# Delta-rule scan: gram products on alternating 64-row halves of TensorE, a padded state operand and one state product per head pair

## The chip, the core and the metric

One core of one Trainium2 chip runs the whole program. The metric is the device time of one execution in microseconds, as the median of several runs.

## The reference, cut to what matters

The program is one inference step of a two-layer model over 640 tokens (128 context tokens and 512 latent tokens, width 1024): layer 0 mixes with a gated linear recurrence, layer 1 with RWKV-7 time mixing, and each layer ends with a mixture of experts. Only the scan of layer 1 is touched. For each of 16 heads of width 64, and in both directions (forwards and backwards over the tokens), it computes the delta rule:

```python
def rwkv7_scan(r, w, k, v, kk, a, s0):
    def step(s, inp):
        r_t, w_t, k_t, v_t, kk_t, a_t = inp
        sa = jnp.einsum('bhvk,bhk->bhv', s, -kk_t)
        s = s * w_t[:, :, None, :] + sa[..., None] * (kk_t * a_t)[:, :, None, :] + v_t[..., None] * k_t[:, :, None, :]
        return s, jnp.einsum('bhvk,bhk->bhv', s, r_t)
```

The kernel computes it in chunks of 128 tokens. Within a chunk the recurrence becomes two masked 128x128 matrices per head and operand pair (gram products of decayed keys, rates and queries), a triangular inverse, and products with the state at the start of the chunk.

## The kernel before

**Tiling of the scan.** Heads are taken in 4 groups `g` of 4 heads (`HG`), which is 2 pairs (`UC`) of 64-wide heads, so that a pair fills 128 partitions: head 0 of a pair lies in partitions 0 to 63, head 1 in 64 to 127. For each group, 5 chunks `st` are taken in order (`st` 0 is the context chunk, which starts from a zero state and has no state product), and in each of these 20 steps both directions `d` are worked on in turn. The loop `for g ... for st` stands three times, once for each engine: TensorE from L980, VectorE from L1981, ScalarE from L1386.

**One step on TensorE**, in program order, always for d = 0 and then d = 1:

- AR (L984) and BR (L992): the gram products. `z["BE"]` or `z["KP"]` (a pair's 128 partitions) is the stationary operand, the moving one is `RHS4`, 512 columns for each pair: head 0's 256 columns hold zeros in partitions 64 to 127, head 1's hold zeros in partitions 0 to 63. A contraction over 128 rows thus gives each head its own product. Two matmuls of 512 columns for a tile.
- AN (L999): bonus sums and the transposes of `KP` and `BE`.
- M0 (L1017): transposes of `N`, and then for levels 1 to 6 the tiles G and D (L1021 to L1047), which build the inverse by doubling. After the G tiles of level 2, `gate_tiles` (L966) makes the gates of the next step: four matmuls that contract over the 64 rows of direction `d`, then one of 256 columns with `bones` over all 128 rows.
- N6 (L1048, transposes), RHS (L1052), Us (L1065), OT (L1074). For `st` > 0, RHS and OT each hold one state product for every head: 128 rows, with the zero halves of `RHS4` as stationary operand and `R0` (64 columns for each pair) as moving one.

**PSUM ring.** There are four PSUM tiles (`RING_P` = 4) that are used in turn. `open_tile(n)` (L661) waits until the reader has freed tile n - 4. M0 for d = 0 therefore takes the place of BR for d = 0, and waits until VectorE has masked that (L2004).

**VectorE in a step**: the mask of AR (L1991) and two operations on `N` (L1997, L1998), for both directions; the masks of BR (L2004); the bonus sums (L2013); `R0` from `ST` (L2016); then the G masks (L2028) and D updates (L2044) of the levels, with the preparation of the next step's operands between and after them, the last of which is `decayed_operands` (L1940), which fills `RHS4` with four operations on 64 partitions. At the end of the step, after each OT tile, it brings up the state (L2071, L2073 or, for `st` 0, L2080), adds the output (L2085) and, from group 1 on, runs `gn_apply` (L1970). All of these stand in one queue in this order.

**ScalarE** copies the transposed tiles (L1393, L1397, L1404, L1429) and computes the gates' exponentials (L1351 and after).

Of the kernel before, what the change touches and what calls it, by code (L numbers as in the profile page):

```python
# [15 lines left out]
P = 128  # L16
D = 1024
KT = D // P
# [23 lines left out]
HG = 4  # L42
# [103 lines left out]
def build(nc, A, const, outs, xspill, slots_in, slots_out):  # L146
# [9 lines left out]
    with ctx:  # L156
# [275 lines left out]
        for d in range(2):  # L432
            z = {}
            for name, n in (("LA", 2 * UW), ("B", UW), ("E1", UW), ("E2", UW), ("E3", UW), ("KK", UW), ("SQ", UW),
                            ("BE", UW), ("KP", UW), ("RHS4_0", 4 * UW), ("RHS4_1", 4 * UW), ("KBT", 2 * UW),
                            ("AR", HG * 256), ("BR", HG * 256), ("M", HG * P), ("N", HG * P), ("G", HG * HD),
                            ("RHU", 2 * HG * HD), ("R0", UC * HD), ("SF", UC * HD)):
# [132 lines left out]
        def _(pool):  # L570
# [87 lines left out]
        def _(pe):  # L658
# [307 lines left out]
            def gate_tiles(g, st):  # L966

                for d in range(2):
                    z, ch, uid = STR[d], chunk_of(st, d), unit_id(g, st, d)
                    lo, ts = slice(HD * d, HD * d + HD), slice(ch * P, (ch + 1) * P)  # L970
                    ps = open_tile(T[f"P_{g}_{st}"] + d)
                    for q, (w2, hid) in enumerate(((W2s, hw), (A2s, ha))):
                        for j in range(UC):
                            ct = UC * g + j
                            mm(ps[:, (UC * q + j) * P:(UC * q + j + 1) * P], w2[lo, ct * P:(ct + 1) * P], hid[lo, ts])
                    pe.wait_ge(S["kk_sq"], uid + 1)
                    done(mm(ps[:, 2 * UW:3 * UW], bones, z["SQ"]))

            gate_tiles(0, 0)
            for g in range(NGRP):  # L980
                for st in range(NCH):
                    u = f"_{g}_{st}"
                    rh = f"RHS4_{(g * NCH + st) % 2}"
                    for d in range(2):  # L984
# [3 lines left out]
                        for j in range(UC):  # L988
                            ins = mm(ps[:, 512 * j:512 * j + 512], z["BE"][:, j * P:(j + 1) * P],
                                     z[rh][:, 512 * j:512 * j + 512])  # L990
                        done(ins)
                    for d in range(2):  # L992
                        z = STR[d]
                        ps = open_tile(T["BR" + u] + d)
                        for j in range(UC):
                            ins = mm(ps[:, 512 * j:512 * j + 512], z["KP"][:, j * P:(j + 1) * P],
                                     z[rh][:, 512 * j:512 * j + 512])
                        done(ins)
# [53 lines left out]
                    for d in range(2):  # L1052
# [3 lines left out]
                        ps = open_tile(T["RHS" + u] + d)  # L1056
# [1129 lines left out]
```

## Time and profile before

| | |
|---|---|
| median of 3 runs | 3113.26 us (3071.8 to 3114.75) |
| span of the profiled execution | 3100.0 us |
| TensorE busy | 2596.5 us, 84% of the span |
| VectorE busy | 1236.9 us, 40% |
| ScalarE busy | 785.9 us, 25% |
| mean granted TensorE clock | 0.902 |
| the 20 steps of the scan (1495.66 to 2620.1 us) | 1124.44 us |

Busy time is counted for each engine on its own. "PE" is TensorE's matmul side, "PEld" its weight loads, which overlap the matmuls, "DVE" is VectorE, "ACT" ScalarE. In a row of the timeline, "x8" is the number of instructions merged into it, and a bracket at its end is the idle time of the engine before it with what released it. "issue" in a bracket means that the profile shows nothing that was waited for. [...]

### The profile page before, as it was taken

How to read it: one execution, taken by the hardware profiler on the slowest of the kernel's cores; microseconds unless marked ns; L12 is line 12 of the kernel's file. 1: busy time of each engine (PE TensorE's matmuls, PEld its weight loads, DVE VectorE, ACT ScalarE, POOL GpSimd, SP SyncE). 2: the span in 40 equal slices, each digit the busy share in tenths (PEclk: the TensorE clock that was granted, in tenths of full speed). 3: DMA queues.
4: the chain of work that ended last, by engine and by line, in shares of the span. 5: the costliest groups of instructions: out<-in, count | busy, mean ns of one | idle time of the engine just before them, and what ended most of it. 6: DMA issues, size and time to landing. Idle time of an engine off the chain costs nothing.

```text
span 3100.0 us, 35206 instructions
## 1 busy us (share of the span) xinstructions
PE 2596.5 (84%) x14506; PEld 1969.5 (64%) x14506; DVE 1236.9 (40%) x2688; ACT 785.9 (25%) x1570; POOL 158.7 (5%) x178
## 2 busy tenths in 40 slices
PE   6999905488899835997799999999999998968974
PEld 3544705455566523556688889888888887556653
DVE  2254126622111116100666665666566665221104
ACT  2253212302011102001334343344243342020111
POOL 2000003400100010001000000000000000000001
PEclk9999956688899967999899997999899999969987
DMA  6144180005699732221000000000000000048962
GB/s 222 55 136 155 56 352 4 2 16 181 232 324 325 229 138 91 68 68 53 3 3 1 1 3 1 1 1 3 1 1 1 3 1 35 28 154 272 346 210 108
DMA packets 202299, 300.99 MB, mean 97 GB/s; under 512 B 12180, under 2 KB 170112, under 8 KB 201760
## 3 DMA queue, kind: packets, MB, share of 16 engines
q1 hardware_dynamic: 180096, 225.62, 22.1%
q0 software_dynamic: 11984, 40.63, 3.5%
q10 hardware_dynamic: 10064, 32.51, 2.6%
q8 instruction: 117, 1.92, 0.3%
q14 instruction: 38, 0.31, 0.0%
HBM read 237.39 MB, written 61.35 MB: 96 GB/s over the span
## 4 chain that ended last, share of the span: by engine, by line
PE 75%; DVE 12%; ACT 3%; DMA 3%; issue 2%; ACTq 2%; POOL 2%; SPq 0%; POOLq 0%; DVEq 0%
PE psum_ring L677 68%; PE psum_ring L1013 4%; DMA arena<-expert_inputs 1%; PE psum_ring L767 1%; ACTq L1263 1%; ACT h_normed L1158 1%; ACTq L1260 1%; ACT arena L1351 1%; DVE arena L1991 1%; DVE x_resid L1991 1%; DVE x_resid L2004 1%; DVE arena L2004 1%; POOL arena L633 1%; POOL expert_inputs L621 1%; DVE h_normed L1829 1%
## 5 line engine op out<-in xcount | busy, mean ns | idle before, releaser
L677 PE MATMUL psum_ring<-arena 128*128 128x64 f32 (+4 forms) x5200 | 982.4, 339 | 54.6 <-ACT arena L1173 17.5
L677 PEld LDWEIGHTS psum_ring<-arena 128*128 128x128 f32 (+1 forms) x5200 | 762.2, 197 | 214.6 <-issue 132.5
L677 PE MATMUL psum_ring<-x_resid 128*128 128x64 f32 x2368 | 334.2, 281 | 0.0
L677 PEld LDWEIGHTS psum_ring<-x_resid 128*128 128x128 f32 x2368 | 306.4, 199 | 0.0
L677 PE MATMUL psum_ring<-arena,weight_ring 128*128 128x512 f32 (+1 forms) x832 | 230.3, 438 | 5.6 <-DVE arena L1804 3.4
L677 PE MATMUL psum_ring<-h_normed,weight_ring 128*128 128x512 f32 (+1 forms) x768 | 211.7, 437 | 5.8 <-ACT h_normed L1158 5.8
L677 PEld LDWEIGHTS psum_ring<-arena,weight_ring 128*128 128x128 f32 x832 | 127.9, 193 | 107.4 <-issue 102.6
L677 PEld LDWEIGHTS psum_ring<-h_normed,weight_ring 128*128 128x128 f32 x768 | 117.8, 192 | 98.9 <-issue 98.8
L677 PE MATMUL psum_ring<-weight_ring,small 128*2 128x256 f32 x768 | 171.9, 382 | 0.0
L677 PE MATMUL psum_ring<-h_normed 128*128 128x128 f32 x190 | 43.4, 411 | 117.5 <-DVE h_normed L1829 98.0
L677 PEld LDWEIGHTS psum_ring<-weight_ring,small 128*2 128x2 f32 x768 | 63.7, 85 | 108.6 <-issue 15.3
L767 PE MATMUL psum_ring<-consts,arena 128*128 128x128 f32 x350 | 56.5, 299 | 90.5 <-DMA arena<-expert_inputs 87.7
L677 PEld LDWEIGHTS psum_ring<-h_normed 128*128 128x128 f32 x190 | 39.3, 311 | 121.6 <-issue 87.9
L767 PEld LDWEIGHTS psum_ring<-consts,arena 128*128 128x128 f32 x350 | 45.6, 154 | 110.2 <-DMA arena<-expert_inputs 90.8
L677 PE MATMUL psum_ring<-x_resid,weight_ring 128*128 128x512 f32 (+1 forms) x320 | 89.9, 444 | 25.7 <-DVE x_resid L1873 25.7
L1183 ACT ACTIVATE arena<-psum_ring 128x256 f32<-128x256 f32 x32 | 12.3, 384 | 368.6 <-PE psum_ring L677 368.6
L1013 PE MATMUL psum_ring<-consts,arena 128*128 128x128 f32 x560 | 91.4, 288 | 14.6 <-DVE arena L2044 14.3
L1404 ACT ACTIVATE arena<-psum_ring 128x512 f32<-128x512 f32 x100 | 59.4, 594 | 170.1 <-PE psum_ring L677 170.1
L1393 ACT ACTIVATE arena<-psum_ring 128x512 f32<-128x512 f32 x40 | 23.9, 598 | 296.8 <-PE psum_ring L1008 296.8
L1013 PE MATMUL psum_ring<-consts,x_resid 128*128 128x128 f32 x560 | 90.9, 287 | 9.3 <-DVE x_resid L2004 9.2
L621 POOL DMA_INDIRECT expert_inputs<-arena x20 | 19.5, 975 | 1476.9 <-DVE arena L1599 1471.4
L1616 DVE TENSOR_TENSOR arena<-arena,psum_ring 128x256 f32<-128x256 f32 x32 | 13.5, 421 | 202.1 <-ACT arena L1183 202.1
(346 smaller groups left out, 3316.8 us busy)
## 6 DMA issues: line engine op xcount, KB each, us to landing
arena<-in_moe_w SPq DMA_DIRECT2D x105, 1024.0 KB, 11.2
weight_ring<-in_w_mod SPq DMA_DIRECT2D x48, 1024.0 KB, 5.4
arena<-expert_inputs SPq DMA_DIRECT2D x35, 512.0 KB, 8.1
expert_outputs<-arena POOLq DMA_DIRECT2D x32, 512.0 KB, 7.8
weight_ring<-in_ab_w_in SPq DMA_DIRECT2D x14, 1024.0 KB, 5.0
expert_inputs<-arena ACTq DMA_DIRECT2D x1, 12800.0 KB, 36.8
expert_outputs<-arena ACTq DMA_DIRECT2D x1, 12800.0 KB, 67.3
weight_ring<-in_ab_w_out SPq DMA_DIRECT2D x4, 1024.0 KB, 6.4
```

The costliest lines, as they stand in the source:

```text
L621: pool.indirect_dma_start(slots_in, bass.IndirectOffsetOnAxis(ap=PI[:, j * NCH + c:j * NCH + c + 1], axis=0), HTOK[:, c, :], None).then_in ...
L633: pool.indirect_dma_start((G0, G1)[j][:, c, :], None, slots_out, bass.IndirectOffsetOnAxis(ap=PI[:, j * NCH + c:j * NCH + c + 1], axis=0)) ...
L677: return nc.tensor.matmul(out, lhsT, rhs, start=start, stop=stop)
L767: ins = nc.tensor.transpose(ps[:, k * P:(k + 1) * P], src[:, k * P:(k + 1) * P], ident)
L1013: ins = nc.tensor.transpose(ps[:, c0 + hl * P:c0 + (hl + 1) * P], src[:, hl * P:(hl + 1) * P], ident)
L1158: A_(H[:, k, a:b], H[:, k, a:b], ACT.Identity, scale=coef[i][:, 2 * k + s:2 * k + s + 1], bias=MOD[:, layer, shift + k, s:s + 1]).then_inc ...
L1260: act.dma_start(dst.rearrange("(a p) d -> p a d", p=P), ZERO.unsqueeze(1).broadcast_to([P, NE + N_OVER, D])).then_inc(S["zero_filled"], 16)
L1263: act.dma_start(outs["rglru"][0, 0].rearrange("d (c p) -> (d c) p", p=P), LROWS[0:8, 0:P]).then_inc(S["lru_sent"], 16)
L1351: ins = A_(z["LA"][:, c0:c0 + P], ps[:, c0:c0 + P], ACT.Exp, scale=-1.0, bias=nb[:, bi:bi + 1])
L1404: A_(STR[d]["N"], ps[:, 512:512 + HG * P], ACT.Copy).then_inc(S["n_out"], 1)
L1991: free(TT(z["AR"].rearrange("p (h c) -> p h c", c=256), ps.rearrange("p (h c) -> p h c", c=256), m, ALU.mult), n)
L2004: free(TT(z["BR"].rearrange("p (h c) -> p h c", c=256), ps.rearrange("p (h c) -> p h c", c=256), m, ALU.mult), n)
```

## The change

- **Operands.** `RHS4_q` (four 128-column parts for each pair, half of it zeros) becomes `RHS_q` (two parts, no zeros). `decayed_operands` fills it with two operations on 128 partitions in place of four on 64.
- **Gram products** (AR, BR). New `gram`: for each pair and each head of it one matmul that contracts over the head's own 64 rows, 256 columns; the calls alternate between rows 0 to 63 and 64 to 127. Head 0's products go to the first PSUM bank of the tile and head 1's to the second, and `masked_gram` on VectorE puts them back in head order as it masks.
- **Gates.** The 64-row matmuls of both directions alternate, and the two `bones` products follow.
- **State products.** `R0` now holds 128 columns for each pair, block-diagonal, with zeros written once by GpSimd. RHS and OT have one state product of 128 columns for each pair in place of one of 64 columns for each head.
- **State on VectorE.** `R0` from `ST`, and `ST` from `R0`, are each two operations on 64 partitions in place of one on 128. GpSimd clears two small tiles in place of four large ones.

```diff
@@ STR tiles
-  ("RHS4_0", 4 * UW), ("RHS4_1", 4 * UW), ... ("R0", UC * HD)
+  ("RHS_0", 2 * UW), ("RHS_1", 2 * UW), ... ("R0", HG * HD)
@@ gpsimd
-                for q in range(2):
-                    nc.gpsimd.memset(STR[d][f"RHS4_{q}"], 0.0).then_inc(S["rw_clear"], 1)
+                nc.gpsimd.memset(STR[d]["R0"], 0.0).then_inc(S["rw_clear"], 1)
@@ tensor, gate_tiles
+                pt = [open_tile(T[f"P_{g}_{st}"] + d) for d in range(2)]
+                for q, (w2, hid) in enumerate(((W2s, hw), (A2s, ha))):
+                    for j in range(UC):
+                        ct = UC * g + j
+                        for d in range(2):
+                            ch = chunk_of(st, d)
+                            lo, ts = slice(HD * d, HD * d + HD), slice(ch * P, (ch + 1) * P)
+                            mm(pt[d][:, (UC * q + j) * P:(UC * q + j + 1) * P], w2[lo, ct * P:(ct + 1) * P],
+                               hid[lo, ts])
                 for d in range(2):
...
+                    pe.wait_ge(S["kk_sq"], unit_id(g, st, d) + 1)
+                    done(mm(pt[d][:, 2 * UW:3 * UW], bones, STR[d]["SQ"]))
+
+            def gram(ps, left, right):
+
+                for j in range(UC):
+                    for hh in range(2):
+                        k = slice(HD * hh, HD * hh + HD)
+                        c0 = (hh * UC + j) * 256
+                        ins = mm(ps[:, c0:c0 + 256], left[k, j * P:(j + 1) * P], right[k, j * 256:(j + 1) * 256])
+                return ins
@@ tensor, AR (BR with z["KP"] alike)
-                        for j in range(UC):
-                            ins = mm(ps[:, 512 * j:512 * j + 512], z["BE"][:, j * P:(j + 1) * P],
-                                     z[rh][:, 512 * j:512 * j + 512])
-                        done(ins)
+                        done(gram(ps, z["BE"], z[rh]))
@@ tensor, RHS (OT alike, with columns P to 2P of the pair's part)
+                        for j in range(UC if st else 0):
+                            mm(ps[:, j * P:(j + 1) * P], z[rh][:, j * 256:j * 256 + P], z["R0"][:, j * P:(j + 1) * P],
+                               j == 0, False)
                         for hl in range(HG):
...
-                            if st:
-                                mm(out, z[rh][:, hl * 256:hl * 256 + P], z["R0"][:, (hl // 2) * HD:(hl // 2 + 1) * HD],
-                                   True, False)
-                            ins = mm(out, z["BR"][:, hl * 256:hl * 256 + P], V1[:, ch, hv], st == 0, True)
+                            ins = mm(out, z["BR"][:, hl * 256:hl * 256 + P], V1[:, ch, hv], st == 0 and hl == 0,
+                                     hl == HG - 1)
@@ vector, decayed_operands
-                for hh in range(2):
-                    pr = slice(HD * hh, HD * hh + HD)
-                    TT(r5[pr, :, hh, 0, :], c3(z["KK"])[pr], c3(z["E3"])[pr], ALU.mult)
-                    ins = TT(r5[pr, :, hh, 1, :], R1[pr, cg, ts], c3(z["E1"])[pr], ALU.mult)
-                ins.then_inc(S["unit_ready"], 1)
+                r4 = z[f"RHS_{(g * NCH + st) % 2}"].rearrange("p (j a t) -> p j a t", j=UC, a=2)
+                TT(r4[:, :, 0, :], c3(z["KK"]), c3(z["E3"]), ALU.mult)
+                TT(r4[:, :, 1, :], R1[:, cg, ts], c3(z["E1"]), ALU.mult).then_inc(S["unit_ready"], 1)
@@ vector, masks of AR and BR
+            def masked_gram(dst, ps, d):
+
+                m = CO[:, C_RMASK + 256 * d:C_RMASK + 256 * d + 256]
+                m = m.unsqueeze(1).unsqueeze(1).broadcast_to([P, 2, UC, 256])
+                return TT(dst.rearrange("p (j h c) -> p h j c", h=2, c=256),
+                          ps.rearrange("p (h j c) -> p h j c", h=2, c=256), m, ALU.mult)
@@ vector, end of a step (R0 from ST is split in the same way)
-                            link(TT(ST[:, KT * d + UC * g:KT * d + UC * (g + 1), :], r0,
-                                    eb.unsqueeze(2).broadcast_to([P, UC, HD]), ALU.mult))
+                            for pr, r0 in state_halves(d):
+                                ins = TT(ST[pr, KT * d + UC * g:KT * d + UC * (g + 1), :], r0,
+                                         eb[pr].unsqueeze(2).broadcast_to([HD, UC, HD]), ALU.mult)
+                            link(ins)
```

## Rows read from the trace of the kernel before

**Rows 1.** The page: busy time of each engine, its share of the span, and instructions.

```profile
PE 2596.5 (84%) x14506; PEld 1969.5 (64%) x14506; DVE 1236.9 (40%) x2688; ACT 785.9 (25%) x1570; POOL 158.7 (5%) x178
```

**Rows 2.** Windows, one scan step each: stretch and length, busy engines, PEclk, DMA, GB/s.

```profile
1819.71:1888.56 68.85, 66.73 (x415) 61.70 (x413) 35.36 (x87) 21.68 (x53) 0.00 (x0) 0.78 0.01 3
1888.56:1952.76 64.20, 62.03 (x415) 56.85 (x414) 36.05 (x90) 21.75 (x53) 0.00 (x0) 0.84 0.00 1
1952.76:2009.20 56.44, 54.25 (x414) 48.92 (x414) 35.77 (x90) 21.65 (x53) 0.00 (x0) 0.97 0.00 1
...
2171.12:2240.20 69.08, 66.91 (x415) 61.73 (x414) 36.04 (x90) 21.75 (x53) 0.00 (x0) 0.78 0.00 1
...
2349.80:2402.35 52.55, 49.68 (x387) 44.22 (x386) 36.04 (x91) 21.65 (x53) 0.00 (x0) 1.00 0.01 1
...
2456.94:2511.74 54.80, 52.61 (x415) 47.28 (x414) 35.67 (x90) 21.65 (x53) 0.00 (x0) 1.00 0.01 1
...
sum 1124.44, PE 1080.40 PEld 973.75 DVE 695.70 ACT 419.68 POOL 0.00; mean PE 54.02 PEld 48.69 DVE 34.78 ACT 20.98 POOL 0.00
```

**Rows 3.** Timeline of TensorE, end of one step (N6, OT) and start of the next.

```profile
2498.30 0.66 PE L1013 MATMUL psum_ring<-consts,arena 128*128 128x128 f32 x4
...
2504.59 4.01 PE L677 MATMUL psum_ring<-arena 128*128 128x128 f32 x34
...
2511.74 7.08 PE L677 MATMUL psum_ring<-arena 128*128 128x512 f32 x16
2518.66 0.50 PE L677 MATMUL psum_ring<-consts,arena 128*128 128x2 f32 x4
...
2520.42 0.63 PE L1013 MATMUL psum_ring<-consts,arena 128*128 128x128 f32 x4
2521.55 0.63 PE L1013 MATMUL psum_ring<-consts,x_resid 128*128 128x128 f32 x4 [0.50 <-DVE x_resid L2004]
```

**Rows 4.** Timeline of VectorE over the same step boundary.

```profile
2511.94 0.58 DVE L2071 TENSOR_TENSOR x_resid<-x_resid,psum_ring 64x128 f32<-64x128 f32 x2 [2.21 <-PE psum_ring L677]
2512.56 0.29 DVE L2073 TENSOR_TENSOR arena<-x_resid,small 128x128 f32<-128x128 f32 x1
...
2513.89 1.22 DVE L1991 TENSOR_TENSOR arena<-psum_ring,consts 128x1024 f32<-128x1024 f32 x1
...
2519.06 1.22 DVE L2004 TENSOR_TENSOR arena<-psum_ring,consts 128x1024 f32<-128x1024 f32 x1
2520.20 1.21 DVE L2004 TENSOR_TENSOR x_resid<-psum_ring,consts 128x1024 f32<-128x1024 f32 x1
...
2521.65 0.28 DVE L2016 TENSOR_TENSOR arena<-arena,small 128x128 f32<-128x128 f32 x1
```

**Rows 5.** Timeline of TensorE around the gate tiles of one step.

```profile
1836.00 1.16 PE L677 MATMUL psum_ring<-arena 64*128 64x128 f32 x8
1837.09 0.70 PE L677 MATMUL psum_ring<-arena,consts 128*128 128x256 f32 x2
1837.72 1.16 PE L677 MATMUL psum_ring<-arena 64*128 64x128 f32 x8
...
1841.98 0.66 PE L1013 MATMUL psum_ring<-consts,arena 128*128 128x128 f32 x4 [0.75 <-DVE arena L2044]
```

**Rows 6.** Timeline of TensorE before and after a stretch at the lower clock.

```profile
1850.06 1.07 PE L677 MATMUL psum_ring<-arena 128*128 128x64 f32 x8 [0.91 <-issue]
...
1880.07 5.35 PE L677 MATMUL psum_ring<-arena 128*128 128x128 f32 x34
```

**Rows 7.** Windows (columns as in rows 2): stretches at the lower clock, the first ahead of the scan.

```profile
1473.00:1480.00 7.00, 6.86 (x34) 5.77 (x34) 1.97 (x4) 1.14 (x4) 0.00 (x0) 0.50 0.02 5
1495.66:1500.60 4.94, 4.94 (x6) 2.19 (x7) 3.28 (x7) 0.00 (x0) 0.00 (x0) 0.50 0.00 0
...
1852.10:1882.90 30.80, 30.80 (x150) 30.74 (x148) 14.47 (x41) 6.63 (x16) 0.00 (x0) 0.50 0.00 1
```

**Rows 8.** Timeline of TensorE ahead of the scan, within the first stretch of rows 7.

```profile
1474.90 2.02 PE L677 MATMUL psum_ring<-arena 64*128 64x128 f32 x8
```

More of the change, by code:

```diff
@@ L982, in _ @@
                     u = f"_{g}_{st}"
-                    rh = f"RHS4_{(g * NCH + st) % 2}"
+                    rh = f"RHS_{(g * NCH + st) % 2}"
                     for d in range(2):
@@ L994, in _ @@
                         ps = open_tile(T["BR" + u] + d)
[L995 to L998, printed above, removed]
+                        done(gram(ps, z["KP"], z[rh]))
                     for d in range(2):
@@ L1084, in _ @@
                                False, True)
+                        for j in range(UC if st else 0):
+                            mm(ps[:, j * P:(j + 1) * P], z[rh][:, j * 256 + P:(j + 1) * 256],
+                               z["R0"][:, j * P:(j + 1) * P], j == 0, False)
                         for hl in range(HG):
@@ L1087, in _ @@
                             hv = slice((HG * g + hl) * HD, (HG * g + hl + 1) * HD)
-                            mm(out, z["BR"][:, hl * 256 + P:(hl + 1) * 256], V1[:, ch, hv], True, False)
+                            mm(out, z["BR"][:, hl * 256 + P:(hl + 1) * 256], V1[:, ch, hv], st == 0 and hl == 0, False)
                             ins = mm(out, z["AR"][:, hl * 256 + P:(hl + 1) * 256], z["U"][:, hl * HD:(hl + 1) * HD],
-                                     False, st == 0)
-                            if st:
-                                ins = mm(out, z[rh][:, hl * 256 + P:(hl + 1) * 256],
-                                         z["R0"][:, (hl // 2) * HD:(hl // 2 + 1) * HD], False, True)
+                                     False, hl == HG - 1)
                         done(ins)
@@ L1880, in _ @@
             read_out(dve, T["stT"] + 1)
-            dve.wait_ge(S["rw_clear"], 6)
+            dve.wait_ge(S["rw_clear"], 4)
             def c3(a):
@@ L1979, in _, with state_halves @@
                     stage(0, 0, d)
+            def masked_gram(dst, ps, d):
[3 more added lines that the diff above has]
+                          ps.rearrange("p (h j c) -> p h j c", h=2, c=256), m, ALU.mult)
+            def state_halves(d):
+                r4 = STR[d]["R0"].rearrange("p (j h v) -> p j h v", h=2, v=HD)
+                return [(slice(HD * hh, HD * hh + HD), r4[HD * hh:HD * hh + HD, :, hh, :]) for hh in range(2)]
             idb = ident.unsqueeze(1).broadcast_to([P, HG, P])
@@ L2065, in _ @@
                         tt = ps[:, 512:512 + UC * P].rearrange("p (j c) -> p j c", c=P)
-                        r0 = z["R0"].rearrange("p (j v) -> p j v", v=HD)
                         eb = em[:, par + 2 * d:par + 2 * d + 2]
                         if st:
-                            for hh in range(2):
-                                pr = slice(HD * hh, HD * hh + HD)
-                                ins = TT(r0[pr], r0[pr], tt[pr, :, HD * hh:HD * hh + HD], ALU.add)
+                            for hh, (pr, r0) in enumerate(state_halves(d)):
+                                ins = TT(r0, r0, tt[pr, :, HD * hh:HD * hh + HD], ALU.add)
                             link(ins)
-                            link(TT(ST[:, KT * d + UC * g:KT * d + UC * (g + 1), :], r0,
-                                    eb.unsqueeze(2).broadcast_to([P, UC, HD]), ALU.mult))
+                            for pr, r0 in state_halves(d):
+                                ins = TT(ST[pr, KT * d + UC * g:KT * d + UC * (g + 1), :], r0,
+                                         eb[pr].unsqueeze(2).broadcast_to([HD, UC, HD]), ALU.mult)
+                            link(ins)
                         else:
```

30 lines of the change are left out of this document (8 added, 22 removed).

## The prediction

> **What bounds the kernel now.** I read the page first. TensorE is busy for 84% of the span and VectorE for 40% [rows 1], so this is a TensorE kernel as a whole. The whole says little about the change, which touches only the 20 steps of the scan. I therefore cut the scan into its steps with the windows view [rows 2]. The reader is to see two things there. A step at the full clock takes 54.8 us from group 1 on (52.55 for the context chunk), of which TensorE is busy for 52.6. And four steps are longer, in step with a lower mean clock: 68.85, 64.20, 56.44 and 69.08 us. Against 54.8 these lose 14.05 + 9.40 + 1.64 + 14.28 = 39.4 us. All 20 steps sum to 1124.4 us.
>
> Next the timelines of TensorE and VectorE over one step boundary [rows 3, 4]. On TensorE the gram products run from 2511.74 to 2518.66, 6.92 us. On VectorE the last output tile of the old step is taken up at 2511.94, and from there its queue has no pause: the state, the output, group normalisation, the mask of AR from 2513.89, the work on N, the other direction, and the first mask of BR from 2519.06, which ends at 2520.28. M0 on TensorE starts at 2520.42, since it needs that PSUM tile. So two chains of nearly equal length end at M0: TensorE's own (grams and AN, 8.7 us) and VectorE's. The second M0 already waits 0.50 us for VectorE [rows 3]. This is what decides the worth of faster grams.
>
> **The change, part by part.** The sum is made against the span of 3100.0 us; the median of the runs, 3113.3, stands 13.3 above it, and I add that at the end.
>
> *State products.* OT of both directions is 64 MATMUL instructions in 7.15 us (2504.59 to 2511.74, rows 3), 0.112 us each, and these are 64 and 128 columns alike, so I price a wider one the same. For each step with `st` > 0, RHS goes from 32 instructions to 24 and OT from 64 to 56. That is 16 x 0.112 = 1.79 us a step, on a stretch where TensorE never waits, and 16 such steps give 28.6 us.
>
> *VectorE at the end of a step.* `ST` is written by two operations. One costs 0.29 [rows 4], a half has as many elements for each partition of its own, so 0.29 more. It stands in the queue ahead of the mask of AR, so M0 comes 0.29 later, 8.97 us after the grams start in place of 8.68: 15 steps, 4.4 us lost. In group 0 there is no group normalisation ahead of the mask, and I take nothing there. `R0` from `ST` becomes four operations in place of two (0.28 each, rows 4). They lie while TensorE does the second M0 and the first G tiles (from 2521.55, about 1.4 us), which covers them; uncovered they would cost 0.6 a step. `decayed_operands` saves four operations a step, in a place where VectorE next waits 2 to 3 us for OT: nothing. GpSimd's clears end ahead of the first gate tile: nothing.
>
> *Gram products, the doubtful term.* 16 instructions of 512 columns become 32 of 256. If the halves of the array don't overlap, they take 6.9 us as now. If they overlap fully, 3.5. No row of before has matmuls on alternating halves. [...] I take 5.1 us, near the middle. A change between 64-row and 128-row matmuls costs about 0.2: eight 64-row ones take 1.09 us to the next kind [rows 5], 8 x 0.112 is 0.90. What the grams save then goes nowhere, for M0 waits for VectorE at 8.97 us: the saved 1.6 us become idle time. With 0.4 for two changes of kind the grams end 5.5 us in, AN runs to 7.1, and TensorE stands idle for 1.9 us, then for another 0.7 ahead of the second M0. Until now it stood 0.5.
>
> [...]
>
> *Gates.* The interleaved order has two changes of kind in place of four, 0.4 us less, more if halves overlap. But TensorE then waits 0.75 us for VectorE [rows 5], which waits for ScalarE's exponentials of both tiles. I take 0; the bound is 0.75 x 19 = 14 us.
>
> *Clock.* At 1849.15 to 1850.06 TensorE idles for 0.91 us among 64-column matmuls, and from 1852.1 the clock is at 0.50 [rows 6, 7]. It stays there for 30.8 us with TensorE always busy, and comes back at 1882.9, within a run of instructions led by 128-column ones on all rows (from 1880.07). The step that holds this is 14.05 us longer, so each microsecond at the lower clock costs 0.456. The idle time of 1.9 and 0.7 us within 5 us is more than the gap that came before that fall, so I expect the fall at M0 in nearly every step. What brings the clock back now? In the first step the grams do: 128 rows and 512 columns, low until 1500.6 and full afterwards [rows 7]. But ahead of the scan, from 1473 to 1480, TensorE is busy for 6.86 of 7.00 us and stays at 0.50; most of that is matmuls of 64 rows [rows 7, 8]. So 64-row matmuls seem to count for less, and the new grams and the gates may fail to raise the clock. The next run of full-row, 128-column work is N6, 41.4 us into a step (2498.30 against 2456.94, rows 2 and 3). From M0 at 9.0 to N6 is 32.4 us of work at the full clock; at the lower one it takes 32.4 / 0.544 = 59.6, so 27.2 us more. I take 18 of 20 steps: 490 us. The 39.4 us of before's own low stretches drop out, as they are in it.
>
> Sum: 3100.0 - 28.6 + 4.4 - 39.4 + 490 = 3526, and 13.3 more: 3540 us.
>
> **The rivals.**
>
> *The clock comes back at the gate tiles.* They hold four 256-column instructions on all rows. For it: these come together now, 0.43 us each at the lower clock. Against it: rows 7, where such pieces between 64-row ones did not do it. Low time is then about 10.6 us of work (M0 at 9.0 to 19.6), 8.9 us more, 18 times 160: 3100 - 28.6 + 4.4 - 39.4 + 160 + 13.3 = 3210.
>
> *The halves don't overlap.* The change then does not do what it says. Grams take 6.9 us plus 0.4, AN ends 9.1 us in, about when VectorE is ready; 0.1 a step, 2 us in all. No new idle time, no fall. But the first step starts low and its grams no longer lift the clock, so it stays low to OT: some 42 us of work, 35 us more. 3100 - 28.6 + 4.4 + 2 + 35 + 13.3 = 3126.
>
> *The clock holds*, the rival on the other side. The idle time opens, but the clock ignores it. For it: dense work lies just before the gaps, while the gap of rows 6 lies among half-filled 64-column work. This is what decides, from the point where the grams' own work carries the stretch around the gap. It gives 3100 - 28.6 + 4.4 + 13.3 = 3089, and 3050 if before's own falls vanish too. [...]
>
> **How the numbers follow.** Overlap of the halves I give 0.78, and a fall of the clock with it about 0.8. The forecast (fall, late return) 0.42, return at the gates 0.20, no overlap 0.22, clock holds 0.16. The likeliest's own range runs from 3400 (14 falls) to 3700 (20 falls and a return only in OT: 47.65 - 9.0 = 38.6 us of work, 32.4 more each). For all cases, 3080 to 3700 leaves out somewhat under half of the last one and a little above, under 0.2; the range is wide since the cases lie far apart. A measurement of this kernel can tell 2% (62 us) from no change. Slower by over that (above 3175) are the first two: 0.62, and 0.01 from the third. Faster (under 3051) is only the edge of the last: 0.06. The rest, 0.31, is within 2%.
>
> **What the profile after would show.** Grams: the time from the first gram instruction to the first of AN, 5.1 us against 6.9 or 3.5. VectorE: no pause from the end of OT to the BR masks, and M0 at 9.0 us. Idle time of TensorE of 1 to 2 us before M0, released by L2004's successor. State products: RHS to the end of OT shorter by 1.8 us in a step at full clock. Clock: a mean near 0.6 to 0.7 over a step, with low stretches that begin at M0 and end in N6 or OT. I am wrong if the clock is full through the levels, if the grams still take 6.9 us, or if the low stretches end at the gates.

## The result, and the profile after

| | before | after |
|---|---|---|
| median, measured together | 3113.13 us (3071.8 to 3114.75, 4 runs) | 3285.26 us (3265.43 to 3304.36, 4 runs) |
| ratio, with its 95% interval | | 1.0598 (1.053 to 1.0666) |
| span of the profiled execution | 3100.0 us | 3267.0 us |
| mean granted TensorE clock | 0.902 | 0.828 |
| 19 steps, first AN to last AN | 1068.4 us | 1223.2 us |

The change makes the kernel 6% slower, 172 us, where 427 us were forecast. The sign came out as forecast, and so did the fall of the clock at M0. The late return of the clock did not, and with it the size: most low stretches end near the gate tiles, which the prediction had named as a sign of being wrong. The time lies in the range (3080 to 3700), but all four cases of the prediction do; it is nearer to the rival in which the clock comes back at the gate tiles (3210) than to the forecast (3540).

The ratios here and below are taken over undisturbed runs of both kernels measured together (before's median lay between 3103.0 and 3113.1 us), so they can differ from the quotient of the medians by up to 1%.

The page of after, first row, answers to [rows 1]: TensorE is busy for 127 us more, and VectorE for 10 less.

```profile
PE 2723.3 (83%) x14570; PEld 2155.0 (66%) x14570; DVE 1226.4 (38%) x2672; ACT 786.9 (24%) x1570; POOL 157.5 (5%) x176
```

Windows of after (columns as in rows 2): four of its steps, and inside two of them the stretch at the lower clock. PEclk, the third number from the end, is TensorE's granted clock as a share of the full one: 1.00 is the full clock, 0.50 the lower level, and a number between the two is a mean over a stretch.

```profile
2051.24:2127.67 76.43, 71.89 (x414) 69.66 (x413) 35.67 (x90) 21.89 (x53) 0.00 (x0) 0.64 0.00 1
...
2263.81:2325.31 61.50, 56.13 (x413) 53.64 (x413) 35.50 (x90) 21.55 (x53) 0.00 (x0) 0.83 0.00 1
2272.30:2289.30 17.00, 16.55 (x82) 15.78 (x83) 6.13 (x17) 4.38 (x10) 0.00 (x0) 0.50 0.00 1
...
2522.77:2581.62 58.85, 54.84 (x414) 52.31 (x413) 34.36 (x86) 21.56 (x53) 0.00 (x0) 0.85 0.01 3
2581.62:2657.81 76.19, 73.11 (x414) 70.83 (x413) 35.77 (x90) 21.89 (x53) 0.00 (x0) 0.62 0.00 1
2589.80:2647.70 57.90, 57.15 (x275) 56.04 (x275) 23.71 (x65) 19.17 (x47) 0.00 (x0) 0.50 0.00 1
```

In [rows 2] a step at the full clock took 54.8 us. In after no step is free of low clock. Where it falls at M0 and comes back some 17 us later (2272.30 to 2289.30), the step takes 58 to 62 us. Where it stays low for 58 us (2589.80 to 2647.70) or falls twice (the first row), the step takes up to 76.

The timeline of TensorE over the start of a step of after answers to [rows 3].

```profile
2581.62 3.72 PE L676 MATMUL psum_ring<-arena 64*128 64x256 f32 x32
2585.27 0.61 PE L676 MATMUL psum_ring<-consts,arena 128*128 128x2 f32 x4
2585.74 0.63 PE L1012 MATMUL psum_ring<-consts,arena 128*128 128x128 f32 x4
2587.83 0.61 PE L676 MATMUL psum_ring<-consts,arena 128*128 128x2 f32 x4 [1.46 <-DVE x_resid L1986]
2588.30 0.63 PE L1012 MATMUL psum_ring<-consts,arena 128*128 128x128 f32 x4
2590.51 1.09 PE L1017 MATMUL psum_ring<-consts,arena 128*128 128x128 f32 x4 [1.58 <-DVE arena L1986]
2591.64 1.09 PE L1017 MATMUL psum_ring<-consts,x_resid 128*128 128x128 f32 x4
```

The reader is to see three things. The grams take 3.65 us (2581.62 to 2585.27) where they took 6.92. TensorE then stands idle twice, 1.46 and 1.58 us, both times for a mask of VectorE (L1986 is `masked_gram`). And M0 starts 8.89 us after the grams, where it was 8.68 before: the step has gained nothing. The clock is at 0.50 from 2589.80, and the same four instructions of M0 take 1.09 us where they took 0.63 [rows 3].

The timeline of VectorE over the same stretch answers to [rows 4].

```profile
2582.34 0.58 DVE L2083 TENSOR_TENSOR arena<-x_resid,small 64x128 f32<-64x128 f32 x2
...
2583.97 1.22 DVE L1986 TENSOR_TENSOR arena<-psum_ring,consts 128x1024 f32<-128x1024 f32 x1
...
2589.15 1.22 DVE L1986 TENSOR_TENSOR arena<-psum_ring,consts 128x1024 f32<-128x1024 f32 x1
2590.28 1.22 DVE L1986 TENSOR_TENSOR x_resid<-psum_ring,consts 128x1024 f32<-128x1024 f32 x1
```

From OT's end to the last mask VectorE has no pause, as before, and a mask costs 1.22 us as before. It is now what M0 waits for by itself. `ST` is two operations (0.58 in place of 0.29).

The granted clock over time, which PEclk averages, shows 29 stretches at 0.50 in after's scan, 624.6 us in sum with the 17.1 us that begin ahead of the first step; before had 5 with 119.5 us, 34.1 of them in the stretch that begins ahead of the first step. I sort those of after by where they begin. In 19 of 20 steps (all but the first) the clock falls 3.3 to 6.2 us after AN's first instruction, between the first of the two waits and 2.1 us behind the start of M0 (4.1 to 5.2 us in); below, that is called a fall at M0. 15 of these stretches end 10.2 to 20.5 us later (245.8 us in sum), three last 58.0 us and the last step's 37.5. Nine more begin later in a step and hold 150.2 us.

The gate tiles stand in 19 of the steps, 18 of them with a fall at M0. In 11 of the 18 the clock comes back during the gate tiles or at most 2.3 us behind the start of their last instruction. In four it is back already 0.7 to 1.0 us ahead of their first instruction (one of them is the 13.7 us from 1620.3), and in all four it falls a second time. In three it stays low through them.

### The profile page after: what moved, and what is told of

Read it like the earlier page. It is cut to its first block, busy times and chain, and to the rows that moved or that the text cites. A ratio compares the mean times of both kernels' runs of the same rounds, so it can differ in the third digit from the quotient of the medians.

```text
span 3267.0 us, 35335 instructions
## 1 busy us (share of the span) xinstructions
PE 2723.3 (83%) x14570; PEld 2155.0 (66%) x14570; DVE 1226.4 (38%) x2672; ACT 786.9 (24%) x1570; POOL 157.5 (5%) x176
## 4 chain that ended last, share of the span: by engine, by line
PE 76%; DVE 12%; ACT 4%; DMA 3%; issue 2%; ACTq 2%; POOL 2%; SPq 0%; POOLq 0%; DVEq 0%
PE psum_ring L676 68%; PE psum_ring L1017 6%; DVE arena L1986 1%; DMA arena<-expert_inputs 1%; PE psum_ring L766 1%; ACT arena L1356 1%; ACTq L1268 1%; DVE x_resid L1986 1%; ACT h_normed L1163 1%; ACTq L1265 1%; POOL arena L633 1%; POOL expert_inputs L621 1%; DVE h_normed L1834 0%; DVE x_resid L2009 0%; DVE arena L2009 0%
## 5 line engine op out<-in xcount | busy, mean ns | idle before, releaser
L676 PE MATMUL psum_ring<-arena 128*128 128x64 f32 (+5 forms) x5472 | 1013.8, 364 | 47.0 <-ACT arena L1178 17.5
L676 PEld LDWEIGHTS psum_ring<-arena 128*128 128x128 f32 (+1 forms) x5472 | 851.7, 226 | 159.8 <-issue 69.2
L676 PE MATMUL psum_ring<-arena,x_resid 128*128 128x64 f32 x2240 | 396.4, 331 | 0.0
L676 PEld LDWEIGHTS psum_ring<-arena,x_resid 128*128 128x128 f32 x2240 | 377.6, 251 | 0.0
L1017 PE MATMUL psum_ring<-consts,arena 128*128 128x128 f32 x1040 | 216.4, 350 | 47.1 <-DVE arena L1986 30.1
L1017 PEld LDWEIGHTS psum_ring<-consts,arena 128*128 128x128 f32 x1040 | 168.1, 198 | 57.3 <-issue 34.5
L2039 DVE TENSOR_TENSOR arena<-psum_ring,consts 128x256 f32<-128x256 f32 x240 | 101.8, 424 | 274.2 <-PE psum_ring L676 273.6
L2055 DVE TENSOR_TENSOR arena<-arena,psum_ring 128x256 f32<-128x256 f32 x240 | 99.4, 419 | 142.3 <-PE psum_ring L676 141.2
L766 PE MATMUL psum_ring<-consts,arena 128*128 128x128 f32 x350 | 56.7, 299 | 90.6 <-DMA arena<-expert_inputs 87.8
L1409 ACT ACTIVATE arena<-psum_ring 128x512 f32<-128x512 f32 x100 | 59.5, 595 | 300.8 <-PE psum_ring L676 300.8
L766 PEld LDWEIGHTS psum_ring<-consts,arena 128*128 128x128 f32 x350 | 45.8, 154 | 110.3 <-DMA arena<-expert_inputs 90.9
L621 POOL DMA_INDIRECT expert_inputs<-arena x20 | 19.5, 974 | 1646.8 <-DVE arena L1604 1641.3
```

Of the source, the lines that this page charges most:

```text
L621: pool.indirect_dma_start(slots_in, bass.IndirectOffsetOnAxis(ap=PI[:, j * NCH + c:j * NCH + c + 1], axis=0), HTOK[:, c, :], None).then_in ...
L676: return nc.tensor.matmul(out, lhsT, rhs, start=start, stop=stop)
L766: ins = nc.tensor.transpose(ps[:, k * P:(k + 1) * P], src[:, k * P:(k + 1) * P], ident)
L1017: ins = nc.tensor.transpose(ps[:, c0 + hl * P:c0 + (hl + 1) * P], src[:, hl * P:(hl + 1) * P], ident)
L1409: A_(STR[d]["N"], ps[:, 512:512 + HG * P], ACT.Copy).then_inc(S["n_out"], 1)
L2039: free(TT(z["G"].rearrange("p (h c) -> p h c", c=HD), ps[:, 0:HG * HD].rearrange("p (h c) -> p h c", c=HD), gm, ALU.mult), n)
```

## The experiments

The expectations name their theories by letters. **A**: the grams take half the time, M0 still waits for VectorE, and the idle time that this opens lets the clock fall. **B**: another part of the change does it, such as the state products or their VectorE work. **C**: it is the 64-row matmuls themselves that count too little for the clock, with or without idle time. D and E concern the order of the gates. The text below quotes what was on record ahead of each run.

One measure goes through all of them: the windows view over the same stretch, 1500 to 2520 us, which holds 13 to 20 steps of each kernel (columns as in rows 2). Here are its rows for before and for after, and a table of all kernels:

```profile
1500.00:2520.00 1020.00, 980.01 (x7329) 882.47 (x7328) 638.96 (x1585) 386.15 (x940) 0.00 (x0) 0.96 0.01 2
```
```profile
1500.00:2520.00 1020.00, 952.46 (x6483) 914.91 (x6482) 544.37 (x1370) 343.08 (x833) 0.00 (x0) 0.77 0.01 1
```

| kernel | median us | ratio (95% interval) | PEclk there | span of the profiled run, us | low clock in the scan, us |
|---|---|---|---|---|---|
| before | 3113.13 | | 0.96 | 3100.0 | 119.5 |
| after | 3285.26 | 1.0598 (1.053 to 1.0666) | 0.77 | 3267.0 | 624.6 |
| e1, grams alone | 3405.14 | 1.1028 (1.0923 to 1.1133) | 0.71 | 3401.9 | 843.1 |
| e2, state alone | 3079.01 | 1.0009 (0.9955 to 1.0063) | 0.96 | 3076.0 | 119.5 |
| e3, after + filler | 3128.48 | 1.011 (0.9973 to 1.0246) | 0.91 | 3117.2 | 235.5 |
| e4, before with half the grams | 3449.94 | 1.1181 (1.1062 to 1.13) | 0.68 | 3446.9 | 969.4 |
| e5, after, gates in the old order | 3414.65 | 1.1098 (1.0983 to 1.1213) | 0.70 | 3388.0 | 904.5 |
| e6, gates alone | 3177.21 | 1.0332 (1.0234 to 1.0429) | 0.87 | 3176.3 | 303.8 |
| e7, after + filler, old gates | 3065.26 | 0.9936 (0.9895 to 0.9978) | 0.97 | 3065.3 | 102.4 |
| e8, after, all grams on one half | 3161.18 | 1.0248 (1.0158 to 1.0339) | 0.86 | 3162.0 | 344.7 |
| e9, e7 with less filler | 3257.89 | 1.0489 (1.0402 to 1.0576) | 0.78 | 3268.3 | 590.5 |
| e10, e7 + one more filler | 3038.89 | 0.9831 (0.9786 to 0.9875) | 1.00 | 3033.9 | 34.1 |

The last column holds the stretches from the one that reaches into the first step to the last that begins before the scan ends. The last two columns go together over all kernels, but for differences of about 25 us that the state products make, and the shortest span is that of the only kernel whose clock never falls in the scan.

**The grams alone (e1).** In before, the new `gram` and `masked_gram`; state products and gates as they were.

```diff
+                        k = slice(HD * hh, HD * hh + HD)
+                        c0 = (hh * UC + j) * 256
+                        r0 = 512 * j + 256 * hh
+                        ins = mm(ps[:, c0:c0 + 256], left[k, j * P:(j + 1) * P], right[k, r0:r0 + 256])
```

> The kernel before with the gram products on alternating halves and their masks alone; state products, state operand and gate tiles as before. Theory A (the grams take half the time, M0 still waits for VectorE, TensorE idles for about 3 us and the clock falls in every step): the clock falls at M0 in all 20 steps, and the time is at or above that of the full change, 3290 to 3450 us, since the gate tiles keep their old order. Rival B (the loss is in the other parts: the block-diagonal state operand, split state writes, the gates' order): 3113 us or less.

Measured: 10.3% slower, more than the whole change. The clock falls 3.0 to 5.7 us after AN's first instruction in all steps but the first, 19 where 20 were expected. Its timeline of TensorE over one step:

```profile
2860.38 1.13 PE L677 MATMUL psum_ring<-arena 64*128 64x256 f32 x8
...
2866.30 0.61 PE L677 MATMUL psum_ring<-consts,arena 128*128 128x2 f32 x4 [1.17 <-DVE x_resid L1988]
...
2868.98 1.08 PE L1017 MATMUL psum_ring<-consts,arena 128*128 128x128 f32 x4 [1.58 <-DVE arena L1988]
```

The same two waits for VectorE, without any other part of the change. The low stretches are longer than in after: 8 of the 19 last 44 us or more (up to 71.7), where in after 3 do.

**The state operand and products alone (e2).** In before, `RHS_q` and the 128-column `R0` beside a padded `RHS4` for the old grams, one state product for each pair, the split operations on `R0` and `ST`.

```diff
+                        for j in range(UC if st else 0):
+                            mm(ps[:, j * P:(j + 1) * P], z[rh][:, j * 256:j * 256 + P], z["R0"][:, j * P:(j + 1) * P],
+                               j == 0, False)
```

> The padded state operand, one state product for each head pair and the split state operations alone. Grams over 128 rows with the zero halves, gate tiles in the old order; both operand layouts are filled, which costs VectorE four operations a step where it has time. Theory A: 16 x 1.79 = 28.6 us less for RHS and OT, 4.4 us more for the split writes of the state, so 3089 us; fewer or more of the kernel's own falls of the clock shift that by up to 40. Rival B: 3200 us or more.

Measured: no change that can be told (1.0009), and a clock of 0.96 as before. The profiled executions make the better comparison, for both hold 119.5 us of low clock: their spans are 3076.0 and 3100.0 us, 24.0 us less, where the sum said 28.6 - 4.4 = 24.2. Its own steps do get shorter. Windows of one step at the full clock, from AN to AN:

```profile
2220.58:2273.90 53.32, 50.89 (x398) 45.50 (x396) 38.34 (x99) 21.69 (x53) 0.00 (x0) 1.00 0.00 1
```

53.3 us against 54.8 from group 1 on, and 52.5 against 54.3 in group 0: 1.5 and 1.8 us less. So B falls. That gain is under half of the difference between two executions of before (3064 to 3130 in these runs), whose mean granted clocks go with their times (0.914 to 0.893).

**Half the gram columns, on full rows (e4).** In before, only 256 of the 512 columns for each pair, contracted over all 128 rows; the masks read them twice. It leaves out the grams of every second head. There is no 64-row gram in it.

```diff
-                            ins = mm(ps[:, 512 * j:512 * j + 512], z["BE"][:, j * P:(j + 1) * P],
-                                     z[rh][:, 512 * j:512 * j + 512])
+                            ins = mm(ps[:, 512 * j:512 * j + 256], z["BE"][:, j * P:(j + 1) * P],
+                                     z[rh][:, 512 * j:512 * j + 256])
```

> The kernel before with only the first 256 of each pair's 512 gram columns computed, over 128 rows; the masks read them twice. It leaves out the gram products of every second head, so its output is not the reference's. TensorE's gram time is halved as in the full change, with no matmul on half the rows. Theory A: the same idle time before M0, falls there in every step, and 3300 us or more although work is left out. Rival C (the 64-row matmuls are the cause): no falls at M0, 3100 us or less.

Measured: 11.8% slower, the slowest of all, with a fall at M0 in 19 steps. Its timeline of TensorE shows M0 behind the same wait:

```profile
1557.01 0.63 PE L1013 MATMUL psum_ring<-consts,arena 128*128 128x128 f32 x4 [1.58 <-DVE arena L2008]
```

Grams of half the time on 128 rows did the same harm (11.8%) as e1's on alternating halves (10.3%). A holds, and C is not needed for the fall.

**The idle time filled (e3).** After, with matmuls in the AN tiles whose result nothing reads: four for d = 0, three for d = 1, each of 256 columns on all rows.

```diff
+                        for _ in range((4, 3)[d]):
+                            mm(ps[:, 256:512], z["KP"][:, 0:P], z["KP"])
```

> The full change with matmuls added that nobody reads: four products of 256 columns over 128 rows into the free columns of the AN tile of direction 0, three into that of direction 1 (0.43 us each, 3.0 us a step), so that TensorE works where it stood idle. Theory A: the clock no longer falls at M0, and 3050 to 3110 us, though work was added. Rival C (64-row matmuls in grams and gates bring the clock down by themselves, idle time or not): falls as in the full change and 3285 us or more.

Measured: 3128.48, 157 us faster than after for seven more matmuls a step, but 18 above what was expected of A. No fall at M0 is left. Its timeline of TensorE over a step:

```profile
2074.12 0.63 PE L1019 MATMUL psum_ring<-consts,arena 128*128 128x128 f32 x4 [0.28 <-DVE arena L1988]
...
2081.95 1.16 PE L676 MATMUL psum_ring<-arena 64*128 64x128 f32 x16
2083.04 1.13 PE L676 MATMUL psum_ring<-arena,consts 128*128 128x256 f32 x4
...
2087.25 0.66 PE L1019 MATMUL psum_ring<-consts,arena 128*128 128x128 f32 x4 [1.35 <-DVE arena L2057]
```

The wait ahead of M0 is down to 0.28 us. A second kind of fall shows behind it, which the expectation had left out. In eight steps the clock now falls 16.5 to 17.6 us after AN, behind the wait of 1.35 us at the end of the interleaved gates. In before that wait was 0.75 [rows 5].

**The gates alone (e6).** In before, the new `gate_tiles` and nothing else.

> The kernel before with the interleaved gate tiles alone. They take about 2.1 us of TensorE in place of 3.3, and the next G tile still waits for VectorE, so the idle time ahead of it grows from 0.75 to about 1.35 us. Theory A (idle time among short matmuls brings the clock down): falls about 17 us after the first AN instruction in some steps, 3110 to 3170 us. Rival: the gates gain what they save, up to 20 us less than before.

Measured: 3.3% slower, a little beyond what was expected. Its timeline of TensorE ahead of a fall at 1874.6:

```profile
1868.28 1.16 PE L677 MATMUL psum_ring<-arena 64*128 64x128 f32 x16
1869.37 1.13 PE L677 MATMUL psum_ring<-arena,consts 128*128 128x256 f32 x4
...
1873.59 0.66 PE L1015 MATMUL psum_ring<-consts,arena 128*128 128x128 f32 x4 [1.35 <-DVE arena L2046]
```

It is the grams' story again, in small: the gate tiles take 2.06 us (1868.28 to the next kind at 1870.34, which is not shown) in place of twice 1.72 [rows 5], the next instruction still waits for VectorE, the wait grows by 0.6, and in 13 of 20 steps the clock falls, in seven of them right there (14.5 to 16.0 us after AN) and in six behind before's old pause.

Where the clock holds, the new order does gain. Windows of one step at the full clock, from AN to AN, of e6 and then of e3:

```profile
2236.63:2290.78 54.15, 51.35 (x414) 46.41 (x413) 35.71 (x91) 21.55 (x53) 0.00 (x0) 1.00 0.00 1
```
```profile
2243.14:2295.78 52.64, 49.57 (x428) 47.32 (x427) 35.32 (x91) 21.55 (x53) 0.00 (x0) 1.00 0.00 1
```

That is 0.65 us less than the 54.8 of before, and 0.7 less than the 53.3 of e10 below, which has the old order: some 13 us over 19 steps, which the falls eat up.

**The gates in the old order, all else new (e5).**

> The full change with the gate tiles in the old order: the 64-row matmuls of direction 0, then its product with bones, then those of direction 1. Theory D (the two halves at work at once are what brings the clock back at the gate tiles): the low stretches that begin at M0 end late, in N6, RHS or OT, in most steps, and the time is that of the grams alone less the 28.6 us of the state products, 3376 us. Rival E (the gates' bones products of 128 rows bring it back, whatever the order): 3285 us as the full change.

Measured: 3414.65, where 3376 was expected by D and 3285 by E. So the new order does harm where the clock is high at the gates (e6), and helps by some 130 us where it is low (3285.26 against 3414.65). The windows of a low stretch of e5, and then its gates within it:

```profile
2017.60:2079.00 61.40, 59.90 (x278) 57.74 (x277) 24.91 (x66) 19.88 (x48) 0.00 (x0) 0.50 0.00 1
```
```profile
2033.21 2.07 PE L676 MATMUL psum_ring<-arena 64*128 64x128 f32 x8
2035.21 1.22 PE L676 MATMUL psum_ring<-arena,consts 128*128 128x256 f32 x2
2036.36 2.07 PE L676 MATMUL psum_ring<-arena 64*128 64x128 f32 x8
```

And the gates of after, at the end of the low stretch 2272.30 to 2289.30:

```profile
2286.47 2.08 PE L676 MATMUL psum_ring<-arena 64*128 64x128 f32 x16
2288.48 1.51 PE L676 MATMUL psum_ring<-arena,consts 128*128 128x256 f32 x4
```

At the lower clock eight 64-row matmuls on one half take 2.0 us (2033.21 to 2035.21), 0.25 each. Sixteen on both halves take the same 2.0 us, 0.126 each. In 11 of the 18 steps of after that have a fall at M0 and gates, the low stretch ends in them or just behind. In e5 none does: in two of 18 steps the clock is back ahead of the gates, in 16 it is low through them, and 12 of the 19 stretches last 44 us or more. E has fallen. What e5 doesn't tell apart is whether the two halves at once raise the clock or the two `bones` products, which the new order puts side by side; in the first grams of after (below) the clock came back after 5.4 us of both halves at once without such products. Three of the four kernels with the new order (after, e3 and e6, not e8) also show the full clock for 3.4 us behind the first gate tiles, ahead of the scan (1476.9 to 1480.3 in after); none of the eight others does.

**Every gram on one half (e8).** After, with every gram contracted over rows 0 to 63: still 64 rows and 256 columns, but never two side by side. It leaves out the true products of every second head.

```diff
-                        k = slice(HD * hh, HD * hh + HD)
+                        k = slice(0, HD)
```

> The full change with every gram product on rows 0 to 63, so that no two run at once; the products of every second head take the wrong rows, so its output is not the reference's. Theory A: the grams take 6.9 us, TensorE has no new idle time before M0, and few or no falls there; with the interleaved gates as they are, 3100 to 3160 us. Rival C (64-row matmuls bring the clock down by themselves): falls within or just behind the grams in most steps, and 3285 us or more.

Measured: 3161.18, just above what A expected (3100 to 3160). Its timeline of TensorE:

```profile
2033.17 7.17 PE L676 MATMUL psum_ring<-arena 64*128 64x256 f32 x32
...
2042.07 0.63 PE L1017 MATMUL psum_ring<-consts,arena 128*128 128x128 f32 x4
2043.20 0.63 PE L1017 MATMUL psum_ring<-consts,x_resid 128*128 128x128 f32 x4 [0.50 <-DVE x_resid L1986]
```

The grams take 7.1 us again, the first M0 waits for nothing and the second 0.50 us as in before, and the clock never falls there. The falls that remain lie at the gates and after, as in e6. So with 64-row grams alone, one at a time, the clock did not fall at M0 in any of e8's 20 steps. But they didn't bring it up either where it was low, in e8's first step. The first step starts low in all kernels. Windows of e8 (one at a time) and of after (both halves), from the first gram on:

```profile
1493.20:1511.50 18.30, 18.27 (x53) 14.81 (x54) 9.23 (x14) 1.20 (x2) 0.00 (x0) 0.50 0.00 0
```
```profile
1492.04:1497.40 5.36, 5.36 (x26) 4.27 (x28) 4.46 (x8) 0.00 (x0) 0.00 (x0) 0.50 0.00 0
```

e8 stayed low through 14.0 us of grams and 4.3 us more of AN and M0, all of it unbroken work, and came back only in M0. After came back within its grams, 5.4 us in. The full rows of before did so 4.9 us in [rows 7]. In all 11 kernels other than e8 the clock is back 3.15 to 6.23 us behind the start of the first gram (e9 and e5), in e8 18.3 us.

**Filler with the old gates (e7).** e3 with the old `gate_tiles`: the change without the idle time that it opened in two places.

> The full change with the unread matmuls in AN (four and three products of 256 columns) and the gate tiles in the old order, so that neither new idle time is left. Theory A: no falls at M0 and none at the gates, a step of 51.7 to 52.6 us at the full clock, and 3040 to 3090 us, less than the kernel before. Rival: the falls at the gates come from something else than the idle time there, and it stays at 3128 us or above.

Measured: 3065.26, 0.6% faster than before. A step at the full clock takes 53.3 us, though, where 51.7 to 52.6 were expected. Nothing falls at M0 or at the gates. What is left are before's own falls, in five of the 14 steps in which the pause of 0.91 us stands, about 27 us after AN. [rows 6] show the pause in before. Here it is again:

```profile
2010.96 1.08 PE L676 MATMUL psum_ring<-arena 128*128 128x64 f32 x8 [0.91 <-issue]
```

**Less filler (e9).** e7 with two and one in place of four and three.

> As the run with the unread matmuls in AN and the old order of the gates, but with two and one of them in place of four and three, 1.3 us a step in place of 3.0, so that about 1.7 us of idle time is left before M0. Theory A (what counts is how much TensorE works around the idle time): falls at M0 in some steps and not in others, and since the gates are in the old order they end late: 3120 to 3300 us. If idle time of any size did it: falls in all steps and 3380 us. If the fall needed the whole 3 us of idle time: 3065 us.

Measured: 3257.89, with falls at M0 in 11 of 20 steps, between none in e7 and 19 in e5 (which has no filler and the same gates). Its timeline shows that the waits are shorter than in after but not gone:

```profile
2249.99 0.70 PE L676 MATMUL psum_ring<-arena 128*128 128x256 f32 x2 [0.59 <-DVE x_resid L1986]
...
2252.67 1.07 PE L1017 MATMUL psum_ring<-consts,arena 128*128 128x128 f32 x4 [1.15 <-DVE arena L1986]
```

The effect grows with the idle time: in most steps from group 1 on, the two waits ahead of M0 are none and 0.28 us in e7 (no fall), 0.59 and 1.15 us in e9 (11 falls), 1.46 and 1.58 us in e5 (19). That is A once more: both other cases on record (falls in all steps, or 3065 us) have fallen.

**Filler ahead of the old pause too (e10).** e7, and one more unread matmul in d = 1's G tile of level 4, just ahead of the 0.91 us.

```diff
+                            if lv == 4 and d:
+                                ins = mm(ps[:, 256:512], z["AR"][:, 0:P], z["AR"][:, 0:256])
```

> As the run with four and three unread matmuls in AN and the old order of the gates, with one more of 256 columns at the end of the level-4 G tile of direction 1, just ahead of the pause of 0.91 us that the profile gives no releaser for. It costs 0.43 x 20 = 8.6 us. Theory A: the falls that follow this pause (five in the profiled execution, 31 us) vanish, and the time is 3040 to 3050 us. Rival: they stay, and 3074 us.

Measured: 3038.89 (3035.14 to 3041.82), 1.7% faster than before and the fastest of all. The pause is down to 0.43 us, with the new matmul in it:

```profile
2265.07 0.65 PE L676 MATMUL psum_ring<-x_resid 128*128 128x256 f32 x2
2266.16 1.08 PE L676 MATMUL psum_ring<-arena 128*128 128x64 f32 x8 [0.43 <-issue]
```

The windows show a full clock over the whole stretch, and a step at 53.3 us:

```profile
1500.00:2520.00 1020.00, 984.57 (x8212) 928.67 (x8208) 665.91 (x1674) 411.69 (x998) 0.00 (x0) 1.00 0.01 2
```
```profile
2240.86:2294.17 53.31, 51.32 (x429) 48.42 (x428) 35.31 (x91) 21.73 (x53) 0.00 (x0) 1.00 0.00 1
```

The step is as long as that of e2: eight unread matmuls a step cost nothing in it, and the parallel grams give nothing. The spread of e10's six runs is 7 us, where before's is 62 in the same comparison.

## Why the prediction was right in sign and wrong in size

**State products and `ST`: right.** 1.79 us less and 0.29 us more a step were forecast, and e2 shows 1.8 less in group 0 and 1.5 less from group 1 on.

**M0 at 8.97 us: right, 8.89.** The faster grams moved nothing but idle time, as forecast.

**Grams at 5.1 us: wrong, 3.65.** The 5.1 was my estimate between 6.9 us (no overlap) and 3.5 (full overlap), and no run shows it. In after's single instructions (grams from 2581.62) all 32 matmuls start in pairs, 6 to 7 ns apart, and a pair follows the last by some 216 ns; the weight loads come in pairs too, 6 to 7 ns apart. In e8, where all grams are on one half, single matmuls follow each other by the same 216 ns. The trace doesn't say on which half an instruction ran, but 32 in 3.65 us, where one half took 7.1 us for them, fit two sequences side by side, with both instructions of one `mm` beside both of the other. 6.92 to 3.65 us is a factor of 1.90. The idle time became 3.04 us where 2.6 was forecast, and lies in part ahead of the second AN. It changed nothing further, since M0 is VectorE's.

**The fall: right.** 18 of 20 steps were forecast, 19 show it. The rival in which the clock holds has fallen. In 11 of the 19 steps TensorE stands idle for 1.46 and 1.58 us (the second wait is 1.50 and 1.35 us in two of them), with 1.1 us of work between; in four, all in group 0, for 0.79 and 1.58 us, and in the four behind a context chunk for 1.58 and at most 0.5 us. The clock fell in all of them, in two (3.3 and 3.5 us after AN) before the second gap had begun. e4 shows the same on full rows: 19 falls, with a wait of 1.27 to 1.58 us in each of these steps.

**Gates at nothing: wrong.** They take 2.06 us in place of 3.4 and lengthen the wait behind them (0.75 to 1.35 us). Where the clock holds that gains 0.65 us a step, close to the bound of 0.75. But alone it costs 3.3% (e6), since the clock falls in the longer wait; a loss was not in the bounds at all. In after the clock comes back at them in 11 steps.

**The return of the clock: the step that failed.** The prediction read [rows 7, 8] as "64-row matmuls seem to count for less, and the new grams and the gates may fail to raise the clock". e8's first step shows this for matmuls that run one at a time: 14.0 us of them left the clock at 0.50. With both halves at once it came back, 5.4 us into after's first grams and, in 11 of 18 steps against none of e5's, in the gate tiles or just behind. And in four steps it was back already 0.7 to 1.0 us ahead of the gates. So the low stretch that was forecast in each of 18 steps, 59.6 us and 1073 in all, came in three steps, and 607.5 us were measured (624.6 without the first 17.1). The rival "comes back at the gate tiles" forecast 19.5 us a step; 15 steps show 16.4 on the mean (245.8 / 15). It is short of the result since it leaves out the three long ones, the last step and the nine later falls, 361.8 us together.

**The price of a low microsecond: too high for these stretches.** 0.456 was taken from one step of before, whose clock fell 25 us after AN. After and e10 differ by 3267.0 - 3033.9 = 233.1 us of span and by 624.6 - 34.1 = 590.5 us of low time, 0.395 for each; e5 against e10 gives 354.1 / 870.4 = 0.41. For falls of the old kind the forecast's price was right: e7, which has no others, gives 31.4 / 68.3 = 0.46 against e10. So the price depends on where the low stretch lies. That TensorE waits for VectorE less while it is slow (it is busy for 57.15 of 57.90 us in after's low stretch 2589.80 to 2647.70, for 52.61 of 54.80 in a full step of before) would explain the difference; no run tests it. With both terms put right, 607.5 x 0.395 = 240 in place of 490, the forecast's sum is 3100.0 - 28.6 + 4.4 - 39.4 + 240 = 3276 against a span of 3267.0. That is no test of the sum, since 0.395 comes from this very span; with e5's 0.41 it is 3285.

**The rest of the sum holds.** Without the clock's term it is 3100.0 - 28.6 + 4.4 - 39.4 = 3036.4. e10, in which the clock never falls, has a span of 3033.9. The lower end of the forecast's own range was added up wrongly: 14 falls of 27.2 us give some 3430, not 3400. Nothing hangs on it.

That the result lies in the stated range is no merit of the forecast: the range was wide enough for every case.

What stays open: why the clock came back ahead of the gates in four steps, at them in 11, and stayed low through them in three. In the three the falls began 4.4 and 4.7 us after AN's first instruction, in others with an early return at 4.0 and 4.8, so the place of the fall doesn't tell them apart.

## What to carry to other kernels

Before a stage of one engine is made shorter, look at what sets the start of the next stage: if that is another engine, the gain is idle time, and it can cost the clock: in after, e1 and e4 every step whose clock fell at M0 has a wait of TensorE of 1.27 to 1.58 us, and these kernels are 6 to 12% slower than before, for the 3.3 us that the grams save in a step. Where the idle time couldn't be used, unread matmuls in it kept the clock at 1.00 from 1500 to 2520 us and cost next to nothing, 53.3 us a step as in e2 without them (e10 is 1.7% faster than before, the change as made 6.0% slower). Most of that 1.7% is the state products and the falls that before had itself; the grams have no part in it. Time the parts of such a change alone, for one of them (the gates) did harm by itself and yet hid half of the harm of another.

## What the runs showed of the hardware that I had not expected

- fp32 matmuls that alternated between rows 0 to 63 and 64 to 127 ran side by side, weight loads included (starts in pairs 6 to 7 ns apart, after): 0.126 us for each instruction against 0.25 at the lower clock (after, e5), and 3.65 against 7.1 us for 32 of 256 columns at the full one (after, e8).
- For raising the clock, 64-row grams on one half did not do in 14.0 us what those on both halves did in 5.4 (e8, after).
- A single pause of 0.91 us among 64-column matmuls was followed by a fall of the clock in five of the 14 steps that have it (e7); with one 256-column matmul in it, which leaves 0.43 us, none of these falls came (e10).
